# Half-length transforms by even and odd times in the long convolution, and its gate convolution moved into the attention

## What is computed

```python
def hyena_mixer(u, conv_w, conv_b, w1, b1, fr1, w2, b2, fr2, w3, b3, skip):
    uc = conv3(u, conv_w) + conv_b               # taps -1, 0, +1 along time, per channel
    x0, x1, vv = jnp.split(uc, 3, axis=-1)       # 512 channels each; x0 is the gate
    zin = x1 * vv
    kern = hyena_filter(L, w1, b1, fr1, w2, b2, fr2, w3, b3)   # 3 small matmuls, 2 sines, a decay
    zf = jnp.fft.rfft(zin, n=2 * L, axis=1)
    kf = jnp.fft.rfft(kern, n=2 * L, axis=0)
    y = jnp.fft.irfft(zf * kf[None], n=2 * L, axis=1)[:, :L]
    return x0 * (y + zin * skip)

for l in range(2):
    xn = rmsnorm(x, norm_mix[l])
    q, k, v, hy, g_a, g_h = split(xn @ w_in[l])
    y_a = window_attention(rope(q), rope(k), v, sink[l]) @ w_attn_branch[l]
    y_h = hyena_mixer(hy, ...) @ w_hyena_branch[l]
    x = x + (sigmoid(g_a) * y_a + sigmoid(g_h) * y_h) @ w_out[l]
    x = x + peer_ffn(rmsnorm(x, norm_ffn[l]), ...)              # 128 x 128 experts, top 16 in 8 heads
```

## Time and profile before

| | |
|---|---|
| median of 3 runs | 3733.85 us (3733.71 to 3734.29) |
| the profiled execution, its time | 3732.75 us |
| its span, first to last instruction | 3731.0 us |
| PE busy | 3535.3 us, 95% of the span |
| DVE busy | 2609.2 us, 70% |
| ACT busy | 1138.0 us, 31% |
| POOL busy | 823.5 us, 22% |
| mean granted clock of PE | 0.977 |
| moved by DMA | 750.49 MB, mean 201 GB/s |

### The profile page before, as it was taken

The page is one execution under the profiler, slowest core; times in us unless marked ns, Lnnn a source line. Parts: engine busy times, 40 slices in busy tenths (PEclk is TensorE's granted clock), DMA queues, the critical chain, the costliest instruction groups (busy, mean ns, idle before and its releaser), DMA issues.

```text
span 3731.0 us, 47726 instructions
## 1 busy us (share of the span) xinstructions
PE 3535.3 (95%) x15818; PEld 2740.4 (73%) x15818; DVE 2609.2 (70%) x5565; ACT 1138.0 (31%) x1748; POOL 823.5 (22%) x661
## 2 busy tenths in 40 slices
PE   6888989999999999999888899899999999999997
PEld 4435855577898898998744367556778889899896
DVE  1454339987888888888724534399878888888887
ACT  1312223355322323323123122133552322323232
POOL 0000004400333333333300000053003333333332
PEclk9989999999999999999999899999999999999998
DMA  3022321455988888888521123213569888888884
GB/s 128 1 77 60 105 75 40 148 204 220 335 303 302 306 309 302 307 299 309 194 103 61 27 64 112 75 61 117 208 255 327 312 302 307 301 304 306 306 300 175
DMA packets 266890, 750.49 MB, mean 201 GB/s; under 512 B 19288, under 2 KB 135768, under 8 KB 239900
## 3 DMA queue, kind: packets, MB, share of 16 engines
q1 hardware_dynamic: 193020, 480.64, 36.2%
q0 software_dynamic: 73760, 268.47, 20.9%
HBM read 684.03 MB, written 65.01 MB: 201 GB/s over the span
## 4 chain that ended last, share of the span: by engine, by line
PE 84%; DVE 8%; ACT 3%; DMA 2%; POOL 1%; issue 1%; DVEq 0%; SPq 0%; POOLq 0%; ACTq 0%
PE ps L982 27%; PE ps L968 20%; PE ps L842 9%; PE ps L920 5%; PE ps L711 5%; PE ps L947 5%; PE ps L892 3%; PE ps L698 2%; PE ps L805 2%; PE ps L830 2%; PE ps L821 1%; DMA URAW<-ut_dram 1%; PE ps L768 1%; PE ps L741 1%; DMA ROWS<-u_rows_dram,GIS 1%
## 5 line engine op out<-in xcount | busy, mean ns | idle before, releaser
L647 POOL DMA_INDIRECT ROWS<-v_rows_dram,GIS x256 | 333.9, 1304 | 577.5 <-DVE X L1760 495.5
L647 POOL DMA_INDIRECT ROWS<-u_rows_dram,GIS x256 | 303.0, 1184 | 614.0 <-DVE STG L1744 519.3
L982 PE MATMUL ps<-VHI,WHI 128*128 128x512 f32 x1536 | 414.6, 392 | 9.3 <-DVE VLO L1713 5.2
L982 PE MATMUL ps<-VLO,WHI 128*128 128x512 f32 x1536 | 416.1, 393 | 0.0
L982 PE MATMUL ps<-VHI,WLO 128*128 128x512 f32 x1536 | 412.4, 391 | 0.0
L1243 ACT CAST VHI<-VRAW 128x512 fp32r<-128x512 f32 x512 | 285.6, 619 | 329.0 <-PE ps L982 329.0
L1250 ACT ACTIVATE AC<-ps 128x384 f32<-128x384 f32 x192 | 94.4, 492 | 945.3 <-PE ps L968 945.0
L920 PE MATMUL ps<-XN,URAW 128*128 128x384 f32 x1024 | 350.5, 490 | 3.3 <-ACTq L381 1.9
L1760 DVE SCALAR_TENSOR_TENSOR X<-ROWS,STG,X 128x1024 f32<-128x1024 f32 x256 | 328.2, 1282 | 21.4 <-DMA ROWS<-v_rows_dram,GIS 7.3
L982 PEld LDWEIGHTS ps<-VLO,WHI 128*128 128x128 f32 x1536 | 289.5, 188 | 63.6
L982 PEld LDWEIGHTS ps<-VHI,WLO 128*128 128x128 f32 x1536 | 289.6, 189 | 62.4
(11 more groups left out here) (244 smaller groups left out, 4855.6 us busy)
## 6 DMA issues: line engine op xcount, KB each, us to landing
VRAW<-v_dram SPq DMA_DIRECT2D x128, 1024.0 KB, 7.3
URAW<-ut_dram SPq DMA_DIRECT2D x128, 512.0 KB, 5.5
URAW<-ut_dram SPq DMA_DIRECT2D x64, 1024.0 KB, 5.8
g_table<-GST SPq DMA_DIRECT2D x12, 4096.0 KB, 12.1
GT<-g_table SPq DMA_DIRECT2D x62, 768.0 KB, 8.1
WR<-w_in_dram SPq DMA_DIRECT2D x8, 2048.0 KB, 13.0
WR<-w_in_dram SPq DMA_DIRECT2D x32, 512.0 KB, 4.6
WR<-w_q_dram SPq DMA_DIRECT2D x8, 2048.0 KB, 8.1
```

The source lines that it names most:

```text
L647: pool.indirect_dma_start(out=ROWS[:, k % GR, :], out_offset=None, in_=table, in_offset=bass.IndirectOffsetOnAxis(ap=GIS[:, par, k:k + 1], ...
L982: last = nc.tensor.matmul(ps[:, 2 + o, :], a[:, par, jj, b * P:(b + 1) * P], c[:, dh, jj, :], start=(first and n == 0), stop=(final and n ...
```

## The change

**Even and odd times.** For the frequency k + 1/2 and its mirror 511 - k, the sum over the even times has the same cosine and the opposite sine, the sum over the odd times the opposite cosine and the same sine. So the table is used for the first 256 frequencies only (`NF` = 2 blocks); PE makes the even part and the odd part of each (`q` = 0, 1, with two blocks `h` of 128 times each), and DVE gets both halves of the spectrum as their sum and difference. Times are picked with every second column (`every_second`) where the filter's last matmul and the turn read their operands. Back, the even times need `YM[:, 0] + YM[:, 1]` and the odd times the difference, and each is one matmul of 256 columns, which reads every second column of the table.

**Copies and sums.** ACT copies two banks at a time, the kernel's even and odd parts to `KFR` (four copies), the input's even part to `ZEV` (two). DVE makes `KF` out of `KFR` with four instructions of 1024 columns, and the product per block `f` is nine instructions of 1024 or 2048 columns.

**Order.** The kernel's transform fills all eight PSUM banks, so the turn waits for its last copy (`kf_copied`). The input's transform no longer waits for DVE. The way back starts with block f = 0 for all `c`, and takes f = 1 when both of its `YF` are there.

**Loads.** `DEC` comes in four transfers, `fwd` in eight (half of the table), `inv` in one (half of it).

**The gate's short convolution** (`X0`) goes in four pieces (`gate_conv`) behind the units 1 to 4 of the attention, for which POOL clears the borders of `HYT` ahead of the barrier. The convolution for `ZT` takes its place between the sines.

```diff
@@ tables and buffers
+NF = NB // 2
+FT_SIZE = NB * 2 * SEQ // 2
+    parts[T_FWD] = 8
-    KF, _ = sb("KF", [P, 2, HC, HW], offset=mrg_at)
+    KFR, _ = sb("KFR", [P, NF, 2, 2, HW], offset=mrg_at)
+    YF, _ = sb("YF", [P, NF, 2, 2, HW], offset=mrg_at)
-    YF, _ = sb("YF", [P, 2, HC, HW], offset=hs_at)
+    KF, _ = sb("KF", [P, NF, 2, 2, HW], offset=hs_at)
+    YM, _ = sb("YM", [P, 2, 2, HW], offset=hyt_at)
+    ZEV, _ = sb("ZEV", [P, NF, 2, HW], offset=hyt_at + 16 * HW)
+    def every_second(x, g):
+        return x.rearrange("p (h i q) -> p q h i", h=2, q=2)[:, g // 2, g % 2, :]
@@ SP
-                sp.dma_start(DEC[:], decay).then_inc(dec_loaded, 16)
-                weights([(lambda s: s, fwd)])
-                weights([(lambda s: s, inv)])
+                for q, s in itertools.product(range(2), range(2)):
+                    sp.dma_start(DEC[64 * s:64 * s + 64, 2 * q:2 * q + 2, :], apart[q, s]).then_inc(dec_loaded, 16)
...
+                weights([even_odd(*qsh) for qsh in itertools.product(range(2), repeat=3)])
+                weights([(lambda w: w[:, 0:NF * 2 * SEQ], inv[:, 0:NF * 2 * SEQ])])
@@ POOL
-                all_at(pool, 1)
                 pool.memset(HYT[:, :, 0:1], 0.0).then_inc(pads_zero, 1)
                 pool.memset(HYT[:, :, SEQ + 1:SEQ + 2], 0.0).then_inc(pads_zero, 1)
+                all_at(pool, 1)
@@ PE
+                def transform(f, q, r, rows):
+                    for h in range(2):
+                        last = nc.tensor.matmul(ps[:, 4 * f + 2 * q + r, :], ft[:, 2 * q + h, r, f * P:(f + 1) * P],
+                                                rows(2 * q + h), start=(h == 0), stop=(h == 1))
+                    return last
+                for f in range(NF):
+                    for q in range(2):
+                        for r in range(2):
+                            last = transform(f, q, r, lambda g: HS[:, r, g, :])
                         last.then_inc(kf_out, 1)
...
+                pe.wait_ge(kf_copied, 2 * NF)
+                for g in range(NB):
                     for c in range(HC):
+                        last = nc.tensor.transpose(ps[:, 4 + g, c * P:(c + 1) * P], every_second(ZT[:, c, :], g), ident)
...
+                vt = WR[:, T_INV % RING, 0:NF * 2 * SEQ].rearrange("p (f r m q) -> p f r q m", f=NF, r=2, q=2)
+                def back(f, c, q):
+                    for r in range(2):
+                        last = nc.tensor.matmul(ps[:, c, q * (SEQ // 2):(q + 1) * (SEQ // 2)], YF[:, f, q, r, c * P:(c + 1) * P],
+                                                vt[:, f, r, q, :], start=(f == q == r == 0), stop=(f == NF - 1 and q == r == 1))
+                    return last
+                for q in range(2):
+                    pe.wait_ge(yf_ready, q + 1)
+                    for c in range(HC):
+                        back(0, c, q)
+                pe.wait_ge(yf_ready, 4)
                 for c in range(HC):
+                    back(1, c, 0)
+                    back(1, c, 1).then_inc(y_out, 1)
@@ ACT
+                for n in range(2 * NF):
                     act.wait_ge(kf_out, n + 1)
+                    nc.scalar.copy(KFR[:, n // 2, n % 2], ps[:, 2 * n:2 * n + 2, :]).then_inc(kf_copied, 1)
...
+                for f in range(NF):
+                    act.wait_ge(zf_out, 2 * f + 1)
+                    nc.scalar.copy(ZEV[:, f], ps[:, 4 * f:4 * f + 2, :]).then_inc(zev_copied, 1)
@@ DVE
+                    normalise(u)
+                    if u == 0:
+                        dve.wait_ge(pads_zero, 2)
+                    if 1 <= u < 1 + HC:
+                        gate_conv(u - 1)
...
-                        short_conv(0, X0)
+                        short_conv(1, ZT)
...
-                short_conv(1, ZT)
...
+                for f in range(NF):
+                    st.did(nc.vector.tensor_tensor(KF[:, f, 0], KFR[:, f, 0], KFR[:, f, 1], ALU.add))
+                    st.did(nc.vector.tensor_tensor(KF[:, f, 1], KFR[:, f, 0], KFR[:, f, 1], ALU.subtract))
+                for f in range(NF):
+                    even, odd = ZEV[:, f], ps[:, 4 * f + 2:4 * f + 4, :]
+                    dve.wait_ge(zev_copied, f + 1)
+                    dve.wait_ge(zf_out, 2 * f + 2)
+                    st.did(nc.vector.tensor_tensor(xb[:, 0], even, odd, ALU.add))
+                    st.did(nc.vector.tensor_tensor(xb[:, 1], even, odd, ALU.subtract))
+                    st.then(dve)
+                    st.did(nc.vector.tensor_tensor(YM[:], xb, KF[:, f], ALU.mult))
+                    st.then(dve)
+                    st.did(nc.vector.tensor_tensor(xb[:, :, 0], xb[:, :, 0], KF[:, f, :, 1], ALU.mult))
+                    st.did(nc.vector.tensor_tensor(xb[:, :, 1], xb[:, :, 1], KF[:, f, :, 0], ALU.mult))
+                    st.did(nc.vector.tensor_tensor(YM[:, :, 0], YM[:, :, 0], YM[:, :, 1], ALU.subtract))
+                    st.then(dve)
+                    st.did(nc.vector.tensor_tensor(YM[:, :, 1], xb[:, :, 0], xb[:, :, 1], ALU.add))
+                    st.then(dve)
+                    nc.vector.tensor_tensor(YF[:, f, 0], YM[:, 0], YM[:, 1], ALU.add).then_inc(yf_ready, 1)
+                    nc.vector.tensor_tensor(YF[:, f, 1], YM[:, 0], YM[:, 1], ALU.subtract).then_inc(yf_ready, 1)
...
+                    vc, zc = (t[:, c, :].rearrange("p (m q) -> p q m", q=2) for t in (VT, ZT))
```

More of the change, by code:

```diff
@@ L19 @@
+import itertools
 import math
@@ L791, in _ @@
                     for i in range(2):
-                        last = nc.tensor.matmul(ps[:, 4 + 2 * (s % 2) + i, :], FR[:, s * P:(s + 1) * P],
+                        last = nc.tensor.matmul(ps[:, 4 + 2 * (s % 2) + i, :], every_second(FR[:], s),
                                                 W3[:, i * HW:(i + 1) * HW], start=True, stop=True)
@@ L797, in _ @@
                 pe.wait_ge(hs_ready, NB)
                 pe.wait_ge(hy_copied, NHY)
-                for f in range(HC):
-                    for r in range(2):
-                        n = 2 * f + r
-                        if n >= 4:
-                            pe.wait_ge(kf_copied, n - 3)
-                        for s in range(NB):
-                            last = nc.tensor.matmul(ps[:, n % 4, :], ft[:, s, r, f * P:(f + 1) * P], HS[:, r, s, :],
-                                                    start=(s == 0), stop=(s == NB - 1))
+                for f in range(NF):
+                    for q in range(2):
+                        for r in range(2):
+                            last = transform(f, q, r, lambda g: HS[:, r, g, :])
@@ L807, in _ @@
                         last.then_inc(kf_out, 1)
                 pe.wait_ge(z_ready, HC)
-                for s in range(NB):
+                pe.wait_ge(kf_copied, 2 * NF)
+                for g in range(NB):
                     for c in range(HC):
-                        last = nc.tensor.transpose(ps[:, 4 + s, c * P:(c + 1) * P], ZT[:, c, s * P:(s + 1) * P], ident)
+                        last = nc.tensor.transpose(ps[:, 4 + g, c * P:(c + 1) * P], every_second(ZT[:, c, :], g), ident)
                     last.then_inc(z_turned, 1)
@@ L814, in _ @@
                 pe.wait_ge(ztok_ready, NB)
-                pe.wait_ge(kf_copied, 2 * HC)
-                for f in range(HC):
-                    if f >= 2:
-                        pe.wait_ge(zf_used, f - 1)
-                    for r in range(2):
-                        for s in range(NB):
-                            last = nc.tensor.matmul(ps[:, 2 * (f % 2) + r, :], ft[:, s, r, f * P:(f + 1) * P],
-                                                    ZTOK[:, s, :], start=(s == 0), stop=(s == NB - 1))
-                    last.then_inc(zf_out, 1)
@@ L824, in _ @@
-                need_tile(pe, T_INV)
-                vt = WR[:, T_INV % RING, :].rearrange("p (f r t) -> p f r t", f=HC, r=2)
-                pe.wait_ge(yf_ready, HC)
-                for c in range(HC):
-                    for f in range(HC):
-                        for r in range(2):
-                            last = nc.tensor.matmul(ps[:, 4 + c, :], YF[:, r, f, c * P:(c + 1) * P], vt[:, f, r, :],
-                                                    start=(f == 0 and r == 0), stop=(f == HC - 1 and r == 1))
-                    last.then_inc(y_out, 1)
+                for f in range(NF):
+                    for q in range(2):
+                        for r in range(2):
+                            last = transform(f, q, r, lambda g: ZTOK[:, g, :])
+                        last.then_inc(zf_out, 1)
@@ L1087, in _ @@
                     nc.scalar.copy(VT[:, 0, :], ps[:, 4 + 2 * (s % 2) + 1, :]).then_inc(h3_copied, 1)
-                for n in range(2 * HC):
+                for n in range(2 * NF):
                     act.wait_ge(kf_out, n + 1)
-                    nc.scalar.copy(KF[:, n % 2, n // 2, :], ps[:, n % 4, :]).then_inc(kf_copied, 1)
+                    nc.scalar.copy(KFR[:, n // 2, n % 2], ps[:, 2 * n:2 * n + 2, :]).then_inc(kf_copied, 1)
                 for s in range(NB):
```

74 lines of the change are left out of this document (40 added, 34 removed).

## The result

| | before | after |
|---|---|---|
| median | 3733.87 us (3733.71 to 3734.29, 4 runs) | 3671.47 us (3669.64 to 3673.32, 4 runs) |
| ratio of after to before | | 0.9834, 95% interval 0.9819 to 0.9849 |
| span of the profiled execution | 3731.0 us | 3671.5 us |
| PE busy, records | 3535.3 us, 15818 | 3470.5 us, 15690 |
| DVE busy | 2609.2 us | 2635.8 us |

The changed kernel is 62.4 us faster; forecast were 67, and the range held the time. A second set of runs of it, beside other runs of before, gave 3670.12 (3667.62 to 3671.94) against 3732.66, ratio 0.9829 (0.9813 to 0.9844).

The account below looks back on a forecast made before the run. PE was taken as the bound, with 84% of the span, and DVE as becoming last in stage B. Terms of -13.8 + 1.4 - 21.1 = -33.5 us a layer, twice -67, gave 3667 us, range 3657 to 3680.

Parts of the forecast that it names:

- The kernel's transform: Stage B on PE: 32 matmuls become 16 at 0.86 us, -13.8 us a layer, with ZT's readiness covered by 6.7 us.
- The new wait: Before the turn in stage B: PE waits for ACT's last copy of two banks, +1.4 us a layer.
- T: PE's start on the input's transform in stage B, from which the later times of the stage were counted.
- DVE becomes last: Product in stage B: DVE needs 11.8 us a block, 23.6 for two, starting 7.27 us after PE's input transform starts.
- The way back and its clock: End of stage B: second half 7.0 us plus 3.0 for a fallen clock; last `c` 41.0 against 62.15, -21.1 us.
- The strided reads: Way back's table read by every second column: taken as free, at most 5.6 us a layer; rival at 1.8, chance 0.09.
- The gate: Gate's convolution moved into DVE's waits in the attention: no cost; rival uncovered, up to 8.3 us a layer, chance 0.04.
- The sum: Per layer -13.8 + 1.4 - 21.1 = -33.5 us, twice -67, giving a median of 3667 us.
- The signs in time: Trace places that would show it: input's transform starting near 251 us, DVE's start on the last `c` near 292.
- the clock didn't stay up between the halves: Rival for the way back: clock stays up in the 2.9 us pause, 3.0 us a layer come back, 3661; chance 0.17.
- it didn't fall in the turn: Rival: clock falls during 4.2 us without a matmul around the turn, +3.0 us a layer, 3673; chance 0.13.
- DVE's new patterns ran at the pace of L437 and not of L417: Slower rival: DVE's product at L417's pace, a block 33.5 us, a layer 10 us more than now, 3754; chance 0.02.

Follow-up runs that it names:

- gate_back: Changed kernel with its short convolutions put back where they were before (the gate's between the sines, the one for ZT behind HS): 3667.81 us.
- dve_plus: Changed kernel with DVE's product of 2048 columns made twice in each spectrum block: 3676.50 us.
- warm_b: Changed kernel with matmuls without use in PE's two pauses, before and between the halves of the way back: 3666.15 us.
- warm_all: Changed kernel with matmuls without use in nine pauses of PE in each layer: 3638.62 us, ratio to before 0.9746.
- warm_before: Kernel before the change with the same matmuls without use, in eight pauses of PE a layer: 3707.57 us.
- inv_plain: Changed kernel with the way back's table laid out as even then odd times, so PE reads neighbouring columns: 3668.11 us.
- shift_before: Kernel before the change with one DVE memset of 1536 columns at the very start: 3733.74 us.
- shift_before2: Kernel before the change with one DVE memset of 3072 columns at the very start: 3734.74 us.
- the split: Changed kernel with DVE's second spectrum block made in two channel halves, PE starting on the first two channel blocks after the first half: 3654.06 us.
- after_again: Changed kernel, unedited, run a second time: 3670.12 us.

## Why the prediction was right, point by point

**The kernel's transform.** Forecast -13.8 us. PE's step took 30.27 us and takes 16.90, -13.4: 16 fewer at 0.86, with 0.4 us more of slow start. `ZT` was ready at 238.0, 8 us before it was asked for. Right, and gate_back shows that the cover was enough even without the move.

**The new wait.** Forecast 1.4 us. The pause is 1.19, the one behind the turn 0.70 in place of 0.89, and the turn 2.16 in place of 1.91 us: together 1.25. Before, the turn also began 0.16 us ahead of the transform's end as the trace models it, so from that end to T it is 4.05 us in place of 2.63, 1.4 more, as forecast. ACT copies 1024 columns in 1.01 us. The 0.25 us in the turn go with the strided weights, which I had set at nothing with 1 us as the upper end; no run takes that stride out.

**DVE becomes last.** Forecast 23.6 us for two blocks, measured 23.8; the first eight matmuls and the lag 7.27, measured 7.27 (249.04 to 256.31). dve_plus shows that this chain sets the end.

**The way back and its clock.** Forecast: second half at T + 31.0, last `c` at T + 41.0. Measured T + 31.09 and T + 41.01. That the second number fits is in part luck, since two sizes in it were off and cancelled: at full clock the second half takes 7.5 us and not 7.0, and its slow start cost 2.4 us and not 3.0 (9.88 against 7.52 in warm_b, which also shows that it was the clock). The first half took 9.09 us, not 10.0, which changed nothing for the end, because PE then waited for DVE. But it made the pause behind it 3.86 us and not 2.9. The stretches over both falls of the clock:

```profile
268.00:268.50 0.50, 0.50 (x3) 0.43 (x2) 0.47 (x2) 0.00 (x0) 0.00 (x0) 0.62 1.17 291
278.00:278.50 0.50, 0.00 (x0) 0.00 (x0) 0.50 (x1) 0.00 (x0) 0.00 (x0) 0.86 0.00 0
```

It fell at 268.12, 0.9 us after PE's restart and 5.1 us after its last stop, and at 278.36, 2.1 us after the next stop. The prediction took the 2.3 and 2.6 us of the kernel before as the time that the clock needs to fall, and that isn't a fixed time. With a pause of 3.86 us the fall came all the same.

**The strided reads.** Set at nothing, between 0 and 5.6 us a layer; measured 0.09 us for each `c`, which is 0.4 us a layer on the second half.

**The gate.** Set at nothing; DVE waits 3.73 us for the scores of unit 3 behind it, where it waited 5.83. Right within 0.6 us a layer (warm_all against warm_before), but the other side of it is that the move brings nothing.

**The sum.** -33.5 us a layer was forecast for stage B, -33.1 and -33.7 are measured. The signs in time came 2 us before their forecast places (the input's transform at 249.0 for 251, the last `c` at 290.1 for 292), because stage B itself began 2.4 us earlier in this trace. The median is 4.5 us above the forecast, and the step that failed is the unsaid one: that the rest of the program keeps its time when a stage is shortened. Of it the rivals had only the clock inside of stage B. The 7.3 us of the trace lie in pauses that, where they are shown, are as long as before and behind which the clock was low for longer; warm_all and warm_before take nearly all of the low clock out of both kernels (20 and 25 us of it are left), and what they take outside of B then agrees within 2 us, all but 0.2 of it from the low clock in D. Shown is that the loss is the clock's. **Open** is why the changed kernel pays more often in those pauses: its code doesn't fix it (inv_plain, gate_back, and the two traces of one program), a later start doesn't bring it to the old kernel (shift_before), and no experiment here ties it to the change. In the traces of before, shift_before and shift_before2 PE works 92 to 95 us at the low clock, in the six traces of the changed kernel and of its edits that have neither fillers nor the split 100 to 127 us.

The rivals: the clock didn't stay up between the halves, it didn't fall in the turn, the gate was covered, and DVE's new patterns ran at the pace of L437 and not of L417. For the turn the stretches show it, over 4.1 us with nothing but transposes and two waits:

```profile
245.00:246.20 1.20, 0.02 (x1) 0.05 (x1) 0.13 (x1) 1.01 (x1) 0.00 (x0) 1.00 0.00 0
246.20:248.30 2.10, 2.10 (x16) 1.95 (x16) 2.10 (x2) 1.36 (x3) 0.00 (x0) 1.00 0.00 0
248.30:249.00 0.70, 0.04 (x1) 0.00 (x0) 0.70 (x2) 0.69 (x2) 0.00 (x0) 1.00 0.00 0
```

That the transposes held the clock up isn't shown by this: in the pause of 4.14 us that follows the input's transform PE does nothing at all, and the clock stayed at 1.00 through it too.

## What to carry to other kernels

When an engine's work is halved and another's doubled beside it, work out the second engine's chain from its own start-to-start times, with each wait on its own result; here that gave the end of the stage to 0.1 us. Then cut the last block of that engine finer, so that the first engine works through it: the split took 9.5 us off stage B in the two layers for the price of nine more instructions in each. And count PE's low clock over the whole program before and after a change: 43 constant matmuls a layer, in pauses that PE has anyway, were worth 32 us here, half of what the change itself brought, and in warm_all's trace the filter, B, C and D to E of the two layers agree within 0.03 us.

## What the runs showed of the hardware

- Weights read with every second column: the loads of the turn took 141 ns each before and 209 ns after, in the groups of the stretch from 150 to 300 us:

```profile
L812 PEld LDWEIGHTS ps<-CST,ZT 128*128 128x128 f32 x16 | 1.8, 141 | 0.5 <-issue 0.5
```

```profile
L838 PEld LDWEIGHTS ps<-CST,ZT 128*128 128x128 f32 x16 | 2.0, 209 | 2.0 <-issue 2.0
```

- A stride of two on the streamed side costs 5% (1.82 us for four matmuls against 1.73, inv_plain), where the Trainium skill (SBUF — State Buffer, "Door 1: The DMA port swizzle") has it free as long as two reads share a 16-byte line. The measurement decides: small, but not nothing.
- A pause of PE of 3.12 us was followed by full clock in one execution of a program and by the low clock in another (after_again and the first trace of the changed kernel). From PE's stop to the fall of the clock 2.1 us passed in one place of stage B and 5.1 us in another, where PE had been back at work for 0.9 us.
- Matmuls of an identity with a constant held the clock: with them the granted clock stayed at 1.00 through all of stage B (warm_all), as it did through both halves of the way back with matmuls on data (warm_b).
